# Products of constant tables on TensorE in the pauses of a fused two-block transformer kernel

## What is computed

```python
def first_block(x, c, ...):
    ada = silu(c) @ ada_w + ada_b                       # six shifts, scales, gates
    h = rmsnorm(x, norm1_g) * (1 + sc1) + sh1
    z = h @ w_in                                        # attention, convolution, gates
    y = (g_attn * (attn @ w_o_attn) + g_conv * (conv @ w_conv_out)) @ w_out
    x = x + gt1 * y
    h = rmsnorm(x, norm2_g) * (1 + sc2) + sh2
    x = x + gt2 * hierarchical_moe(h, ...)              # top group, top 2 of its 8 experts
    return rmsnorm(x, final_norm_g)

def second_block(x, c, ...):
    for i in range(2):
        h = rmsnorm_2(x, norm_w[i]) * (1 + scale) + shift
        y = gdn_mixer(h, ...) if i == 0 else fox_mixer(h, ...)
        x = x + gate * y
    return rmsnorm_2(x, final_norm_w)
```

## Time and profile before

| | |
|---|---|
| Time, median of 3 runs | 1213.63 us (1212.24 to 1217.85) |
| Profiled execution, own time | 1212.93 us |
| its span, first to last instruction | 1211.1 us |
| TensorE matmuls busy | 1088.7 us, 90% of the span, 8142 records |
| VectorE busy | 628.2 us, 52% |
| ScalarE busy | 493.5 us, 41% |
| GpSimd busy | 401.4 us, 33% |
| DMA | 186.2 MB, mean 154 GB/s |
| Granted clock of TensorE, mean over the span | 0.937 |

### The profile page before, as it was taken

One profiled execution on the slowest core, in us unless ns is written; L12 is line 12 of the kernel. 1 busy time (PEld: TensorE's weight loads), 2 busy tenths in 40 slices (PEclk: granted clock), 3 DMA queues, 4 the chain that ended last, 5 costly groups with the idle time before them and its releaser, 6 DMA issues. The chain is left out here.

```text
span 1211.1 us, 20112 instructions
## 1 busy us (share of the span) xinstructions
PE 1088.7 (90%) x8142; PEld 929.3 (77%) x8142; DVE 628.2 (52%) x1366; ACT 493.5 (41%) x1103; POOL 401.4 (33%) x337
## 2 busy tenths in 40 slices
PE   5899778998999999998799989999889978999986
PEld 1796577788767777776788889899779868788866
DVE  4689965364433455555464435544453434455553
ACT  1635333502211011014386656736744534565532
POOL 0551433020000000113376465455443426455421
PEclk9799889898899999998799989999989988899987
DMA  9524340776099999614023212222211213333301
GB/s 366 199 92 178 108 170 13 301 303 241 22 378 359 402 391 396 254 70 178 35 105 107 71 70 82 95 81 97 78 63 56 86 40 138 105 109 135 106 35 35
DMA packets 25867, 186.22 MB, mean 154 GB/s; under 512 B 4144, under 2 KB 4912, under 8 KB 5680
## 3 DMA queue, kind: packets, MB, share of 16 engines
q1 hardware_dynamic: 24192, 184.77, 40.0%
q10 hardware_dynamic: 432, 0.18, 0.1%
q0 software_dynamic: 1152, 0.00, 0.0%
HBM read 196.46 MB, written 1.05 MB: 163 GB/s over the span
## 5 line engine op out<-in xcount | busy, mean ns | idle before, releaser
L2983 POOL TENSOR_TENSOR wL<-ring,wH 128x512 fp32r<-128x512 f32 x210 | 282.8, 1360 | 317.0 <-ACT wH L1535 316.5
L683 PE MATMUL bank<-xH,wH 128*128 128x256 f32 x800 | 253.4, 317 | 16.2 <-DVE xL L2144 12.3
L683 PE MATMUL bank<-xH,wL 128*128 128x256 f32 x800 | 234.8, 293 | 0.0
L683 PE MATMUL bank<-xL,wH 128*128 128x256 f32 x800 | 234.2, 293 | 0.0
L683 PEld LDWEIGHTS bank<-xH,wH 128*128 128x128 f32 x800 | 161.8, 202 | 31.1 <-issue 23.1
L683 PEld LDWEIGHTS bank<-xH,wL 128*128 128x128 f32 x800 | 162.3, 203 | 4.6 <-issue 4.3
L683 PEld LDWEIGHTS bank<-xL,wH 128*128 128x128 f32 x800 | 161.8, 202 | 0.0
L1535 ACT ACTIVATE wH<-ring 128x512 fp32r<-128x512 f32 x264 | 154.7, 619 | 17.3 <-DMA ring<-in_wts 9.7
L683 PE MATMUL bank<-ring,xg 128*128 128x256 f32 x640 | 145.6, 381 | 2.4 <-DMA ring<-in_exw 2.4
L683 PEld LDWEIGHTS bank<-ring,xg 128*128 128x128 f32 x640 | 119.5, 190 | 25.0 <-DMA ring<-in_exw 5.5
L2144 DVE SCALAR_TENSOR_TENSOR sz<-ring,cact,sz 128x512 f32<-128x512 f32 x154 | 124.6, 809 | 11.7 <-DMA ring<-in_wts 7.7
(11 more groups left out here) (205 smaller groups left out, 1893.5 us busy)
## 6 DMA issues: line engine op xcount, KB each, us to landing
ring<-in_wts SPq DMA_DIRECT2D x123, 1024.0 KB, 5.0
ring<-in_exw SPq DMA_DIRECT2D x32, 1536.0 KB, 9.2
ring<-in_wts SPq DMA_DIRECT2D x1, 1152.0 KB, 5.0
xT<-in_xT SPq DMA_DIRECT2D x1, 1024.0 KB, 11.6
out<-hT SPq DMA_DIRECT2D x4, 256.0 KB, 2.6
cst<-in_cst SPq DMA_DIRECT2D x1, 800.0 KB, 15.7
ring<-in_wts SPq DMA_DIRECT2D x1, 640.0 KB, 3.6
vec<-in_vec SPq DMA_DIRECT2D x1, 217.0 KB, 5.8
```

The costliest lines, as they stand in the source:

```text
L683: return pe.matmul(o, l, r, start=start, stop=stop, skip_group_check=True)
L2983: return pool.tensor_tensor(o, x, h.bitcast(F32), ALU.subtract)
```

## The change

A helper `warm(b, n)` issues n matmuls of the table of ones by the first 256 columns of the tables (the identity and the ones) into PSUM bank b. They are plain float32, no semaphore tells of their end, and nothing reads their results: the next real matmul into the bank overwrites them. `bank(b)` inside makes them wait for the earlier readers of the bank. `warm` is called at twelve places of the list of TensorE, ahead of waits; nothing else is altered. Counted out, these are 89 matmuls: 11 in the loop of `route`, 3 before the ranks, 4 before `gather`, 5 in `project(3)`, 5 in `decayed(0)` of each of four groups, 6 and 2 in `out_proj("bo", 0 and 1)`, 2 in each of the last four heads, 4 before the last scatter, 10 behind its norm sums, 10 before and 6 behind the last `out_proj("ao")`.

```diff
--- before.py
+++ after.py
@@ -686,6 +686,12 @@
                 n = a.shape[0]
                 return pe.transpose(o, a, cst[0:n, CIDX["ident"]:CIDX["ident"] + n])
 
+            def warm(b, n):
+
+                p = bank(b)
+                for _ in range(n):
+                    mm(p[:, 0:256], C("ones"), cst[:, 0:256])
+
             def three(p, wh, wl, xh, xl, start, stop):
                 mm(p, wh, xh, start, False)
                 mm(p, wl, xh, False, False)
@@ -970,6 +976,7 @@
                 e.wait_ge(loaded("rt"), "rt")
                 p, t = [bank(q) for q in range(2)], [bank(3 + i) for i in range(4)]
                 for k in range(8):
+                    warm(2, 4 if k == 0 else 1)
                     e.wait_ge(norm_a, (1, k))
                     for q in range(2):
                         i = mm(p[q][:, 0:36], hT[:, k, 128 * q:128 * q + 128], w[:, k, :], k == 0, k == 7)
@@ -984,6 +991,7 @@
                     for h in range(2):
                         until(3 + 2 * h + q, (hk_d, (h, q)))
                 p, oh = bank(7), routed("g_oh")
+                warm(2, 3)
                 e.wait_ge(rt_d, "g3")
                 mm(p[:, 0:4], C("triU"), oh[:, 0, :])
                 mm(p[:, 4:8], C("triU"), oh[:, 1, :], True, False)
@@ -1114,6 +1122,8 @@
                     if s in (1, 5):
                         i = s // 4
                         p = bank(2)
+                        if (g, i) == (3, 1):
+                            warm(2, 5)
                         e.wait_ge(pn_a, (g, i, 0))
                         mm(p[:, :], C("ones"), sqn[:, :]).then_inc(pn_p.up((g, i)))
                         until(2, (pn_a, (g, i, 1)))
@@ -1247,6 +1257,8 @@
                 def decayed(c):
                     q, r0 = c // 2, 64 * (c % 2)
                     p = bank(7)
+                    if c == 0:
+                        warm(7, 5)
                     e.wait_ge(cs_d, (g, f"v{c}"))
                     for i in range(4):
                         m = mm(p[:, 128 * i:128 * i + 128], kdc[r0:r0 + 64, i, q, :], vnw[r0:r0 + 64, q, i, :])
@@ -1308,6 +1320,8 @@
                 yield
 
             def out_proj(name, g, u, last=False):
+                if name == "bo":
+                    warm(0, 2 if g else 6)
                 for n in range(8):
                     wn = f"{name}{g}" + "ab"[n // 4]
                     wh, wl = parts(wn, 4)
@@ -1419,6 +1433,8 @@
                 yield
                 yield
                 p = bank(5)
+                if g == 3:
+                    warm(5, 2)
                 e.wait_ge(fh_r, (h, 2))
                 for j in range(3):
                     m = tr(p[:, 128 * j:128 * j + 128], Pb[n][:, 128 * j:128 * j + 128])
@@ -1469,6 +1485,7 @@
             columns()
 
             route()
+            warm(2, 4)
             gather()
             gad = chain(*[ada(j) for j in range(10, 24)])
             for u in range(42):
@@ -1489,10 +1506,12 @@
                 if 11 <= u and (u - 11) % 8 < 4:
                     scatter((u - 11) // 8, (u - 11) % 8)
             columns()
+            warm(1, 4)
             for i in range(4):
                 scatter(4, i)
             for k in range(8):
                 stat(2, k, 2)
+            warm(1, 10)
 
             gd = decays()
             weave(project(0), (gd, 0.5))
@@ -1512,7 +1531,9 @@
             nx = out_proj("ao", 2, 3)
             weave(back(3), (nx, 1.2))
             each(nx)
+            warm(0, 10)
             with_stats(out_proj("ao", 3, 3, True), 3, 6)
+            warm(0, 6)
 
             gd = forgets()
             weave(fox_project(0), (gd, 0.2))
```

## The result

| | before | changed |
|---|---|---|
| Median | 1214.45 us (1212.24 to 1217.85, 4 runs) | 1198.84 us (1194.59 to 1204.81, 4 runs) |
| Profiled execution, own time | 1212.93 us | 1204.81 us |
| its span | 1211.1 us | 1203.0 us |
| Granted clock, mean over the span | 0.937 | 0.961 |

The ratio is 0.9886, with a 95% interval from 0.9855 to 0.9916: faster by 1.1%. Two later comparisons of the same two kernels gave 0.9852 (0.9822 to 0.9882) and 0.9893 (0.9875 to 0.9910). The forecast was 1200, the range 1192 to 1213. The profiled execution of the changed kernel is the slowest of its four.

A forecast was written before the change was run, and what follows sets the result against it. Pauses were taken to cost twice, by their length and by TensorE's half clock in the dense work behind them. Terms -3.0 + 1.5 + 0 - 5.6 - 2.2 - 3.6 + 0 = -12.9 from 1212.93 gave 1200 us, range 1192 to 1213.

The forecast's parts named there:

- Slower: Rival, all filled places: products of constant tables don't keep the clock and only add cost; 1229.7 us, chance 0.08.
- Price of a product: Each added product: 0.46 us at full clock, 0.84 at half; free if it ends within the pause.
- Router, -3.0: Router: loop a draw at full clock, three products 0.3 us late, ranks 1.0 and gather 2.3 us back.
- I let the gain pass: Experts behind the router: TensorE stays busy and loads wait for its slots, so the router's -3.0 us is kept.
- swallowed: Rival, recurrence and router: savings become waits for VectorE, ScalarE or loads, losing 5.6 and 3.0 us; 1208.6 us, chance 0.17.
- Last scatter, +1.5: Before the last scatter: four products at half clock end 2.9 us late, about half made up; bounds +0.5 and +2.9.
- Norm and decays, 0: Behind the last scatter's norm sums: ten products free, but TensorE waits for GpSimd; 0, bounds -2 and +0.5.
- Recurrence, -5.6: back(0) to (3) and project(3): products free, 8.0 us to win behind them, 0.7 of it kept; bounds -8.0 and -2.
- Last "ao": Last "ao" projection: ten products free, dense stretch at 979.8 runs at full clock, -2.2 us; six behind it, 0.
- "bo" 0: First "bo" projection and last heads: six products free, stretch at 1153.9 gives -4.5, first head costs +0.9; -3.6 us.
- "bo" 1: Second "bo" projection: two products in short pauses, clock falls again nearby; 0, bounds -2 and +1.5.
- All of it: Rival: all nine stretches behind filled pauses run at full clock and TensorE alone decides; 1186.7 us, chance 0.10.

The follow-up runs named there:

- e2_narrow: Changed kernel with all 89 products one column wide instead of 256; 1215.83 us, ratio 1.0016 to the kernel before.
- e8_double: Changed kernel with every count of products doubled, 178 in all; 1216.42 us, ratio 1.0028 to the kernel before.
- e4: Changed kernel without the seven products within the router's loop; 1191.03 us, ratio 0.9844 to the kernel before.
- m3: Changed kernel without router-loop products, last scatter's four ahead of columns(), more pauses filled in decays, first projection, front(g); 1189.75 us, ratio 0.9789 to the kernel before.
- m4: As m3, plus products in the first layer before conv_in and the attention heads' softmax waits; 1181.08 us, ratio 0.9728 to the kernel before.
- e1_router: Kernel before plus only the 18 products of the router, in route and before gather; 1211.30 us, ratio 0.9969 to the kernel before.

## Why the prediction was right or wrong, point by point

1. **What bounds the kernel, and the double price of a pause.** Right. e2_narrow puts products of one column at the same places and wins nothing; with 256 columns the kernel wins 1.1 to 1.5%. That is the rival "Slower" answered: products of constant tables kept the clock.
2. **Price of a product, 0.46 us.** Right: eight records in 1.97 us and a loop that is 0.43 us longer a step, at half clock eight records in 3.2. The products that end within a pause cost nothing (waits of 0.73, 0.73 and 0.49 us were left). For those beyond it I took the whole price; e8_double says 0.19 us, since much of TensorE's work there is paced by others.
3. **Router, -3.0.** Right in size: -3.2 to -3.3 in all six traces that have these products, with the loop's eight steps 8.07 us long against 8.2. Wrong in what it said of the cause: the clock would not have fallen without the loop's products, and these cost 3.0 us that the loop could have saved (6.41 against 9.43 us). I had taken the products for what holds it; the filled pause ahead was enough, in three traces (e4, m3, m4).
4. **"I let the gain pass" through the experts.** Half wrong. The step took the experts for bound by TensorE alone. Their section grew by 1.1 to 5.9 us, by a new fall near 320 and by loads. By time e1_router still won 0.15 to 0.46%, but over the seven traces only about 1 of the 3.2 us is left behind the experts. The rival "swallowed" is largely true here.
5. **Last scatter, +1.5.** Mis-sized: +2.05 in one trace, -0.93 in four. I took the fall's place in the one trace for fixed. It moves from execution to execution, and where it lies earlier the products bring the clock back for the scatter.
6. **Norm and decays, 0.** Nearly right as the sections go (+0.73, a little over my upper bound of +0.5, and +0.03), and for its reason: GpSimd paces TensorE. But it was not the limit: with a product in each of these waits m3_more took 3.1 us out, as the narrow matmuls and the dense ones behind them then run at full clock.
7. **Recurrence, -5.6.** Right within its bounds: -5.0 alone, -4.4 on average over seven traces, from -1.9 to -6.6. By time it is 5.8 to 11 us, more than the 5.6. The part given back went to a new fall in front(3), not to longer waits as I wrote.
8. **Last "ao", -2.2.** Right: -2.25 and -2.24.
9. **"bo" 0, -3.6; "bo" 1, 0.** -4.1 in the section that holds the first, -1.9 in the second, which was within its bounds of -2 and +1.5: the fall at 1181 is gone, and the clock stays up to 1200. I had priced the products of the last heads as a cost alone. Whether they or the two of "bo" 1 did it, no run tells, since all runs have both or neither.
10. **The sum.** -12.9 against -8.1 in the profiled execution and -15.6 by the medians. That 1200 lies so near the median is in part luck, since errors cancel: the experts took back most of the gain that I had let pass, and the end of the kernel gave 2.4 us more than I counted. What separates executions of one kernel lies mostly where nothing was changed: the first layer's 292.07 us are 293.74, 293.38 and, in other runs, 287.8 to 297.1, and the attention layer's three us of difference are falls that come or don't. A forecast from one trace doesn't see this spread.

"All of it" (1187) did not come, because falls moved as well as went: 44 of 106 us at half clock stayed. m4_more_first, with most pauses filled, has four stretches left behind 290 us, 17 us together, and comes to 1181.

## What to carry to other kernels

Where TensorE pauses for some us and dense work follows, look for half clock in that work, and count only the part of it in which TensorE decides; matmuls of constant tables, sized to end just before the wait does, gave that part back here at no cost. Fill the pause ahead of a run of small matmuls, not the run itself, and look for the falls that come later in the same stage: in the recurrence one came 12 to 13 us on, until m3_more filled the small pauses there too. Products that end a little late cost less than their length where another engine paces what follows.

## What the runs showed of the hardware

- Small work did not raise the clock, however busy the engine looked: all of 13.5 us busy with matmuls of 1 to 128 columns, all at half clock (e2_narrow). Once high, the clock can stay high through small work, as in the 6.4 us of the router's loop in e4_no_loop, or fall, as behind 3.8 us of matmuls of 16 columns in the kernel before (at 1017.4).
- Float32 transposes of 128 columns kept the clock as matmuls did: 0.9862 with them, 0.9852 to 0.9893 with products. In both the operands were constant: ones, or ones and identity.
- Changing nothing before 287 us, executions of kernels with the same first layer reached the router between 287.8 and 297.1 us. The time at half clock in it goes from 34 to 48 us, and the layer is mostly longer with it (287.8, 287.9 and 288.7 with 34, 293.7, 297.0 and 297.1 with 48); but e8_double took 293.8 with 34, so it isn't all. Why the falls differ stays open.
